# The last mixer's attention: units of two heads in one branch instead of two branches of one head, and a new order of ScalarE's work

## The reference, cut to what matters

```
def query_block(qb):
    p_c = masked_softmax(qn . kc_blk, ...)             # compressed branch: 31 keys
    o_c = p_c @ vc_blk
    p_s = masked_softmax(qr . k_sel, kpos <= t)        # selected branch
    o_s = p_s @ v_sel
    p_w = masked_softmax(qr . kwin, window of 512)     # window branch
    o_w = p_w @ vwin
    o = g[0] * o_c + g[1] * o_s + g[2] * o_w
```

## Time and profile before

| | us |
|---|---|
| median of 3 runs (2641.0 to 2654.1) | 2651.84 |
| the profiled execution's own time | 2643.49 |
| its span, first to last instruction | 2641.7 |
| the changed stage, from 2002.5 to 2200.9 | 198.4 |

### The profile page before, as it was taken

The page is one execution under the profiler, slowest core; times in us unless marked ns, Lnnn a source line. Parts: engine busy times, 40 slices in busy tenths (PEclk is TensorE's granted clock), DMA queues, the critical chain, the costliest instruction groups (busy, mean ns, idle before and its releaser), DMA issues. The chain is left out here.

```text
span 2641.7 us, 32435 instructions
## 1 busy us (share of the span) xinstructions
PE 2393.4 (91%) x13850; PEld 1834.6 (69%) x13850; DVE 999.5 (38%) x1577; ACT 724.8 (27%) x1234; POOL 233.6 (9%) x255
## 2 busy tenths in 40 slices
PE   6978999988999989995789999999986777999997
PEld 3535556777888868884767888877864555788886
DVE  2013118534332326745133433423335443342333
ACT  2123200123222223313223322322113443342331
POOL 0003107300000000012000000000022430000000
PEclk8989999999999998986579999998987998999999
DMA  7120004311222112100012222212110003222210
GB/s 292 36 83 33 32 32 160 128 64 64 80 112 96 72 73 96 64 32 3 3 68 92 96 96 96 96 67 96 66 32 1 1 1 128 79 102 99 102 66 32
DMA packets 17119, 196.35 MB, mean 74 GB/s; under 512 B 2000, under 2 KB 3152, under 8 KB 5072
## 3 DMA queue, kind: packets, MB, share of 16 engines
q1 hardware_dynamic: 15824, 189.67, 19.3%
q10 hardware_dynamic: 1152, 4.61, 0.4%
HBM read 190.08 MB, written 2.10 MB: 73 GB/s over the span
## 5 line engine op out<-in xcount | busy, mean ns | idle before, releaser
L1585 DVE TENSOR_TENSOR wsp_mlp<-ring,wsp_mlp 128x1024 fp32r<-128x1024 f32 x128 | 156.8, 1225 | 438.6 <-ACT wsp_mlp L1547 438.6
L1547 ACT CAST wsp_mlp<-ring 128x1024 fp32r<-128x1024 f32 x128 | 134.3, 1049 | 349.8 <-PE psum L1532 345.4
L1529 PE MATMUL psum<-hs_mlp,wsp_mlp 128*128 128x512 f32 x512 | 201.9, 394 | 8.1 <-DVE hs_mlp L1418 8.1
L1529 PE MATMUL psum<-acts_mlp,wsp_mlp 128*128 128x512 f32 x512 | 202.4, 395 | 0.0
L1531 PE MATMUL psum<-hs_mlp,wsp_mlp 128*128 128x512 f32 x512 | 201.4, 393 | 0.0
L1532 PE MATMUL psum<-hs_mlp,wsp_mlp 128*128 128x512 f32 x512 | 201.1, 393 | 0.0
L1532 PE MATMUL psum<-acts_mlp,wsp_mlp 128*128 128x512 f32 x512 | 199.4, 389 | 0.0
L1531 PE MATMUL psum<-acts_mlp,wsp_mlp 128*128 128x512 f32 x512 | 199.3, 389 | 0.0
L1585 DVE TENSOR_TENSOR wsp_ffn<-ring,wsp_ffn 128x1024 fp32r<-128x1024 f32 x66 | 80.9, 1225 | 236.5 <-ACT wsp_ffn L1547 236.5
L424 PE MATMUL psum<-hsev,wspev 128*128 128x512 f32 x672 | 158.2, 398 | 3.9 <-DVE wspev L404 3.9
L424 PEld LDWEIGHTS psum<-hsev,wspev 128*128 128x128 f32 x672 | 129.6, 193 | 32.1 <-DVE wspev L404 4.7
(11 more groups left out here) (423 smaller groups left out, 4159.7 us busy)
## 6 DMA issues: line engine op xcount, KB each, us to landing
ring<-weights SPq DMA_DIRECT2D x85, 2048.0 KB, 7.9
ring<-weights SPq DMA_DIRECT2D x3, 1024.0 KB, 4.9
cst<-consts ACTq DMA_DIRECT2D x1, 2209.0 KB, 14.5
xT<-xin SPq DMA_DIRECT2D x2, 1024.0 KB, 6.8
ring<-weights SPq DMA_DIRECT2D x1, 1280.0 KB, 5.9
mixT<-ctxin ACTq DMA_DIRECT2D x1, 1024.0 KB, 15.1
ring<-weights SPq DMA_DIRECT2D x2, 512.0 KB, 3.5
arena<-arena_low SPq DMA_DIRECT2D x8, 128.0 KB, 2.3
```

The source lines that it names most:

```text
L1529: pe.matmul(tile_bank(g, j), w_hi, src[:, 0, k0 + i, :], start=(first and i == 0), stop=False)
L1547: act.copy(wsp[:, q % 2, 0, :], raw_view(q)).then_inc(s["w_hi"], 1)
L1585: dve.tensor_tensor(wsp[:, q % 2, 1, :], raw_view(q), wsp[:, q % 2, 0, :].bitcast(F32), ALU.subtract).then_inc(s["w_lo"], 1)
```

## The change

A unit `w` is now one step in one branch, with both heads: 64 units again, numbered `2v + br`. Scores of a unit are two products and use two of the four banks (those of the branch). They wait only for the exponentials of unit w-2. The values are also split by branch, and the compressed branch's four products stand in the second half. The orders by hand are:

- TensorE, for unit w: scores of unit w+2, values of unit w-1, transposes of unit w.
- VectorE, for unit w: reciprocal of unit w+1, row minima of unit w+2, copy of unit w.
- ScalarE, for unit w: (at units 9, 17, ... the store of the pair that ended), copy of unit w, exponentials of unit w+2.
- GpSimd: as before, by the new units.

The row minima and the transposes signal after each head, no longer after two, so ScalarE can start on head 0 while head 1 is under way.

```diff
+        def part_of(w):
+            return steps[w // 2] + (w % 2,)
...
-                def scores(v):
-                    t, j, i = steps[v]
-                    if v >= 1:
-                        pe.wait_ge(exp_done, 2 * v)
-                    for br in range(2):
+                def scores(w):
+                    t, j, i, br = part_of(w)
+                    if w >= 2:
+                        pe.wait_ge(exp_done, w - 1)
+                    for par in range(2):
+                        rows = slice(64 * par, 64 * par + 64)
+                        last = pe.matmul(bank(2 * br + par, (i + 1) * P), qr[rows, 4 * t + j, i * P:(i + 1) * P],
+                                         kr[rows, 2 * br + t, 0:(i + 1) * P], start=True, stop=True)
+                    last.then_inc(score_done, 1)
+
+                def turn(w):
+                    i = part_of(w)[2]
+                    pe.wait_ge(prob_done, w + 1)
+                    if w >= 1:
+                        pe.wait_ge(turn_a, w)
+                        pe.wait_ge(turn_v, w)
+                    for par in range(2):
+                        for k in range(i + 1):
+                            last = pe.transpose(bank(turn_bank(w, par))[:, k * P:(k + 1) * P],
+                                                pp[:, w % 4, par, k * P:(k + 1) * P], ident)
+                        last.then_inc(turn_done, 1)
+
+                def values(w):
+                    t, j, i, br = part_of(w)
+                    pe.wait_ge(turn_a, w + 1)
+                    pe.wait_ge(turn_v, w + 1)
+                    if br == 0 and i == 0 and w >= 8:
+                        pe.wait_ge(pv_out, w // 8)
+                    blk = slice(32 * j, 32 * j + 31)
+                    for k in range(i + 1):
                         for par in range(2):
...
                 scores(0)
-                for v in range(NV):
-                    if v + 1 < NV:
-                        scores(v + 1)
-                    if v >= 1:
-                        values(v - 1)
-                    turn(v, 0)
-                    turn(v, 1)
-                values(NV - 1)
+                scores(1)
+                for w in range(NW):
+                    if w + 2 < NW:
+                        scores(w + 2)
+                    if w >= 1:
+                        values(w - 1)
+                    turn(w)
+                values(NW - 1)
...
+                lows(0)
+                lows(1)
                 inverse(0)
-                inverse(1)
-                for v in range(NV):
-                    if v + 1 < NV:
-                        lows(v + 1, 0)
-                        lows(v + 1, 1)
-                    out(2 * v)
-                    if v + 1 < NV:
-                        inverse(2 * v + 2)
-                    out(2 * v + 1)
-                    if v + 1 < NV:
-                        inverse(2 * v + 3)
+                for w in range(NW):
+                    if w + 1 < NW:
+                        inverse(w + 1)
+                    if w + 2 < NW:
+                        lows(w + 2)
+                    out(w)
...
                 exps(0)
                 exps(1)
-                for v in range(NV):
-                    if v + 1 < NV:
-                        exps(2 * v + 2)
-                    out(2 * v)
-                    if v + 1 < NV:
-                        exps(2 * v + 3)
-                    out(2 * v + 1)
-                    if v % 4 == 0 and v >= 4:
-                        store(v // 4 - 1)
+                for w in range(NW):
+                    if w % 8 == 1 and w >= 8:
+                        store(w // 8 - 1)
+                    out(w)
+                    if w + 2 < NW:
+                        exps(w + 2)
                 store(7)
```

More of the change, by code:

```diff
@@ L2628, in program @@
         steps = [(t, j, i) for t, j in pairs2 for i in range(TT)]
-        NV = len(steps)
+        NW = 2 * len(steps)
         score_done, low_done, exp_done, inv_done, prob_done = (
@@ L2632, in program, with turn_bank @@
         turn_done, turn_a, turn_v, pv_done, pv_out = (sem(n) for n in ("turn2", "turn_a2", "turn_v2", "pv2", "pv_out2"))
-        def turn_bank(u, br):
-            return 4 + (2 * u + br) % 3
+        def part_of(w):
+            return steps[w // 2] + (w % 2,)
+        def turn_bank(w, par):
+            return 4 + (2 * w + par) % 3
         with nc.Block() as block:
@@ L2639, in _ @@
             def _(pe):
-                def scores(v):
-                    t, j, i = steps[v]
-                    if v >= 1:
-                        pe.wait_ge(exp_done, 2 * v)
-                    for br in range(2):
-                        for par in range(2):
[L2646 to L2683, removed]
+                def scores(w):
[7 more added lines that the diff above has]
+                    last.then_inc(score_done, 1)
@@ new lines, in values @@
+                def values(w):
[6 more added lines that the diff above has]
+                    for k in range(i + 1):
+                        for par in range(2):
+                            g = 2 * t + par
+                            out = psum[64 * par:64 * par + 64, 7 * 512 + i * P:7 * 512 + (i + 1) * P]
+                            last = pe.matmul(out, vtok[:, k, br * 256 + g * ND:br * 256 + (g + 1) * ND],
+                                             pT[w % 4][:, par, k, :], start=(br == 0 and k == 0), stop=False)
+                    if br == 1:
+                        for par in range(2):
+                            g = 2 * t + par
+                            out = psum[64 * par:64 * par + 64, 7 * 512 + i * P:7 * 512 + (i + 1) * P]
+                            last = pe.matmul(out, vcb[blk, g * ND:(g + 1) * ND], pcT[blk, g, i * P:(i + 1) * P],
+                                             start=False, stop=True)
@@ L2696, in _ @@
+                values(NW - 1)
             @block.vector
             def _(dve):
[L2698 to L2717, removed]
+                def lows(w):
+                    i, br = part_of(w)[2:]
+                    dve.wait_ge(score_done, w + 1)
+                    n = (i + 1) * P
+                    for par in range(2):
+                        s = bank(2 * br + par, n)
+                        dve.tensor_tensor_reduce(out=s, in0=s, in1=later[:, T - n:T], scale=1.0,
+                                                 scalar=-NEG, op0=ALU.add, op1=ALU.min,
+                                                 accum_out=st2[:, w, par:par + 1]).then_inc(low_done, 1)
@@ new lines, in inverse, with out @@
+                def inverse(w):
+                    dve.wait_ge(exp_done, w + 1)
+                    dve.reciprocal(st2[:, w, 4:6], st2[:, w, 2:4]).then_inc(inv_done, 1)
+                def out(w):
+                    i = part_of(w)[2]
+                    dve.wait_ge(turn_done, 2 * w + 2)
+                    if w >= 4:
+                        dve.wait_ge(pv_done, w - 3)
+                    dve.tensor_copy(pT[w % 4][:, 1, 0:i + 1, :],
+                                    bank(turn_bank(w, 1), (i + 1) * P).rearrange("p (k n) -> p k n", n=P))\
@@ L2722, in _ @@
                 dve.wait_ge(later_set, 2)
-                lows(0, 0)
-                lows(0, 1)
+                lows(0)
+                lows(1)
                 inverse(0)
-                inverse(1)
-                for v in range(NV):
-                    if v + 1 < NV:
-                        lows(v + 1, 0)
-                        lows(v + 1, 1)
-                    out(2 * v)
-                    if v + 1 < NV:
-                        inverse(2 * v + 2)
-                    out(2 * v + 1)
-                    if v + 1 < NV:
-                        inverse(2 * v + 3)
+                for w in range(NW):
[4 more added lines that the diff above has]
+                    out(w)
@@ L2738, in _ @@
             @block.scalar
             def _(act):
[L2740 to L2748, removed]
-                    last.then_inc(exp_done, 1)
@@ L2751, in out, with exps @@
[L2751 to L2757, removed]
+                def exps(w):
+                    i, br = part_of(w)[2:]
+                    if w >= 4:
+                        act.wait_ge(turn_done, 2 * (w - 4) + 2)
+                    n = (i + 1) * P
+                    for par in range(2):
+                        act.wait_ge(low_done, 2 * w + par + 1)
+                        last = act.activation(pp[:, w % 4, par, 0:n], bank(2 * br + par, n), ACT.Exp,
+                                              bias=st2[:, w, par:par + 1], scale=-1.0,
+                                              accum_out=st2[:, w, 2 + par:3 + par])
+                    last.then_inc(exp_done, 1)
@@ L2759, in store, with out @@
+                def out(w):
+                    i = part_of(w)[2]
+                    act.wait_ge(turn_done, 2 * w + 1)
+                    if w >= 4:
+                        act.wait_ge(pv_done, w - 3)
+                    act.copy(pT[w % 4][:, 0, 0:i + 1, :],
```

(12 more changed lines are left out.)

## The result

The changed kernel takes 2624.38 us (median of 7 runs, 2618.47 to 2633.08) against 2645.46 for the kernel before in 7 runs: a ratio of 0.9913, 95% interval 0.9888 to 0.9937. The forecast was 22 us less; the interval is 17 to 30 less. In absolute terms it was 2629.8 us, worked out from a median of 3 runs of the kernel before (2651.84); over 7 runs that median is 2645.46. The profiled execution took 2625.66 us.

The account below looks back on a forecast made before the run. Bound by handovers between engines (a scores-minima-exponentials ring) and clock drops, no engine full. Stage 13.5 + 147.0 + 14.6 = 175.1 against 198.3 us; with one drop left 22 less, so 2651.84 becomes 2629.8 us, range 2609 to 2648.

Parts of the forecast that it names:

- TensorE's work, 18.6 us in a pair: One pair of heads: 17.1 us of products and transposes, plus 1.5 for the fixed part of twice as many groups.
- The waits, 2.4 us: Waits left on TensorE in a pair: 0.55, 0.50, 0.28 for copies of units 5 to 7, 1.06 for the store.
- What goes: Scores' wait for exponentials, with at least 1.0 us slack, and a turn's wait for copies before it, both gone.
- The sum: Whole stage: 13.5 us start, 147.0 for seven pairs, 14.6 end; 175.1 against 198.3 if no drop remains.
- The size of a drop: Each fall to half clock, seen at block 3's scores, costs some 1.5 us; one of five was taken to remain.
- The two parts of the gain: Stage 23.2 us shorter if no drop remains, 15.7 if all five stay with 7.5 us lost; one left, 22.
- The signs: Stage 170 to 183 us, pairs 21, clock above 0.95; wrong if pairs exceed 22 or middle blocks show half clock.
- A reading that was short: Profile before: TensorE waits 21.1 us for copies before the second head's transposes.
- The lower bound: No fixed part for the extra groups and no drop: 10 us more gained, a gain of 32.
- The first rival: The five clock drops stay as they are: only 15.7 us less, 2636 us; chance 0.12.
- The second: VectorE's exponentials, reciprocal, minima, copy, values, turn set the pace: pair 24.0 us, 2649 us; chance 0.11.
- The slower rival: Clock sinks and stays low in blocks 2 and 3, units 4 to 7: 63 us slower, 2715; chance 0.05.

Follow-up runs that it names:

- One set of banks: Changed kernel with scores of a unit waiting for exponentials of unit w-1, not w-2, the banks staying four: 2747.57 us, 1.0385 of the kernel before.
- the repeat: The changed kernel run again unaltered beside the kernel before: 2625.0 us, ratio 0.9923, stage 177.1 us, one clock drop.
- early store: Changed kernel with the store of a finished pair one unit earlier in ScalarE's order: 2622.1 us, 0.9903 of the kernel before.
- minima first: Changed kernel with the early store, plus VectorE's minima of unit w+2 ahead of the reciprocal of unit w+1: 2613.66 us, 0.9875 of the kernel before.
- units of one head: Changed kernel's orders and banks, but a unit is one head with its two branches: 2722.86 us, 1.0292 of the kernel before.
- three changes of order: Changed kernel with early store, minima first, and head 0 turned ahead of values in each pair's last unit: 2608.59 us, again 2611.44; 0.9854 and 0.9873 of before.
- the filler ahead: Three changes of order plus 11 unread products in each of three waits just ahead of the stage: 2607.48 us, 0.9852 of the kernel before.

## Why the prediction was right

- **TensorE's work, 18.6 us in a pair**: 21.11 less 2.30 of waits is 18.8 as the rows print them. The prediction counted groups without their tail of 0.07 us; on that count the four waits are 2.58 and the work is 18.5. The split groups pay their fixed part: scores of block 3 take 2043.52 - 2042.46 = 1.06 us for half the products against 1.92 for all, so 0.20 is fixed, where 0.23 was taken.
- **The waits, 2.4 us**: 0.55, 0.50, 0.28 and 1.06 were walked; 0.51, 0.45, 0.24 and 1.10 came at the places named, or 0.58, 0.52, 0.31 and 1.17 on the prediction's count.
- **What goes**: the wait for exponentials. At the end of the stretch shown, block 1's exponentials ended at 2055.21 and the scores that reuse their banks started at 2056.57. But the slack was overrated: the walk had at least 1.0 us, and between the first exponentials of block 2 and the first scores of block 3 only 0.62 us are left, 2039.64 - 2039.02:

```profile
2038.81 0.21 ACT L2743 ACTIVATION_READ_ACCUMULATOR arena<-psum,arena_low 128x1 f32 x1
...
2039.64 1.13 PE L2649 MATMUL psum<-arena_low,arena 64*128 64x512 f32 x4
```

  It is 1.0 to 2.0 us at the other units. One set of banks brings the wait back and makes the kernel slower than before.
- **The sum**: start 13.6 us (13.5 forecast), seven pairs 150.8 (147.0), end 14.7 (14.6). The 3.8 us too many are 0.8 for pairs of 21.11 and 3.0 for one drop.
- **The size of a drop** was off: I took 1.5 us, from the earlier trace rows, for the one left. In the changed kernel it costs 24.14 - 21.11 = 3.03 us, for it lasts 6.5 us, all of them dense work. In the kernel before a drop lasted 3.3 us and doubled only block 3's scores. Why it lasts longer here stays open.
- **The two parts of the gain**: five drops cost 7.4 us before and one costs 3.0 now, so the clock gives 4.4 us of the first profile's 19.0 and the waits and the split groups together 14.6. The prediction had 6.0 and 15.7.
- So the stage gave 19.0 us in the first profile and 21.1 in the second, where 21.7 was worked out; 2.0 of that difference is a shorter cold start, which the change doesn't touch. The medians of whole executions gave 21.1, and 21.1 again in the repeat. With intervals of 13 us, and a sum whose errors are 3.8 us in one stage, that they come within 1 us of the forecast is in part luck.
- **The signs**: those of the waits, the pair and the stage came. The clock in the stage is 0.94 in the first profile, not above 0.95, with a cold start of 13 us, and 0.96 in the second, with 8.5 us. And half clock did appear once in the middle blocks, which had been named as a sign of being wrong: the drop covers the scores of block 2, not those of block 3 as before.
- **A reading that was short**: TensorE's 21.1 us for copies are those of ScalarE alone. For VectorE's copies it waited another 11.9 us:

```profile
PE psum L2661 <- DVE arena_low L2716: 11.9, 15, 1.0
```

- **The lower bound** does not follow from its terms: 1.5 us less in each of eight pairs and no drop are 13.5 us, not 10.
- **The first rival** (drops stay) did not come: five went down to one. In all six profiles of the changed units without the 1.10 us wait there was none behind the cold start, in 42 pairs, and both drops of the changed kernel came right behind that wait, in 2 of 14 pairs. That the wait causes them is likely, not shown.
- **The second** (VectorE's order becomes the ring) is real as a part of the waits: beside the early store, minima first takes 0.53 us from a pair. It never set the pair.
- **The slower rival** (the clock stays low) did not come here, though it is no fancy: in one set of banks it took 5 to 9 us of each pair, and in units of one head 13 us of two pairs.
- **ScalarE's order**, which the change's title names, is not where the gain is: turned round, it gives the same whole time and a pair shorter by 0.45 us.

## What to carry to other kernels

When every engine is half idle, look for the ring that one set of buffers closes, and count TensorE's own work in it: that work is the floor that the pair comes near when the buffers are doubled (here 18.8 us of work in pairs of 21.11). Then walk one period in each engine's written order and note what stands behind each waiting instruction; the small late ones (a store behind exponentials, a reciprocal ahead of minima) could be worked out to about 0.1 us each in the changed kernel, and three changes of order gave 1.57 us in a pair, as much as the change itself (22.74 to 21.11). The walks of the experiments came out less well: the early store was to give 1.10 us and gave 0.71. When work is cut into units, keep in one unit what TensorE can do side by side.

## What was not expected of the hardware

- With units of one head, whose score and value products use one half of TensorE's rows or columns at a time, a pair ran at a granted clock of 0.68 over 42.3 us in which TensorE was busy for 41.3, and the next pair, the same work, ran at 1.00 in 29.7. Why some pairs fall and others don't stays open.
- A pair at full clock repeats within 0.02 us, in every kernel that had one. Where one kernel was profiled twice, the spread of its stage is the clock's but for 0.1 us: its drops, and the cold start, which lasts 8.5 to 14 us from the stage's first product. It lasts 6 where the filler ahead had lifted the clock for a while, and 30 and 36 in the two slower kernels.
- 1.0 us of work whose result nobody reads, put into a wait of 1.3 us once in each of eight pairs, made the stage of the kernel before 7.4 us shorter.
